# Time-mix preparation of a two-block network on one core: units of k moved among the low-rank products, PSUM banks named by hand, and VectorE's and ScalarE's order rewritten

## The reference, cut to what matters

```python
xs = x[None] + mu[0] * dx_prev + mu[1] * dx_next             # six mixtures of x with its neighbours
r, k, v = einsum('ibld,ide->ible', xs[:3], w_rkv)
lw = tanh(xs[3] @ w1[n]) @ w2[n]                             # n = 0, 1: the two directions, rank 64
decay = exp(-exp(-softplus(-(w0 + lw)) - 0.5))
a = sigmoid(a0 + (xs[4] @ a1[n]) @ a2[n])                    # rank 64
g = sigmoid(xs[5] @ g1) @ g2                                 # rank 160
kk = k * k_k ; kk = kk / max(sqrt(sum over a head of kk*kk), 1e-12)
kd = k * (1 + (a - 1) * k_a)
```

## Time and profile before

| | before |
|---|---|
| median of 3 runs | 2629.68 us |
| profiled execution | 2632.66 us |
| its span | 2630.8 us |
| TensorE busy | 2520.9 us, 96% |
| VectorE busy | 1975.1 us, 75% |
| ScalarE busy | 1532.5 us, 58% |
| mean granted clock of TensorE | 0.981 |

### The profile page before, as it was taken

One profiled execution on the slowest core, in us unless ns is written; L12 is line 12 of the kernel. 1 busy time (PEld: TensorE's weight loads), 2 busy tenths in 40 slices (PEclk: granted clock), 3 DMA queues, 4 the chain that ended last, 5 costly groups with the idle time before them and its releaser, 6 DMA issues. The chain is left out here.

```text
span 2630.8 us, 47726 instructions
## 1 busy us (share of the span) xinstructions
PE 2520.9 (96%) x20277; PEld 2086.0 (79%) x20277; DVE 1975.1 (75%) x2831; ACT 1532.5 (58%) x2229; POOL 175.8 (7%) x192
## 2 busy tenths in 40 slices
PE   8999999999997999999999999999999999999998
PEld 7779997688976667676676767666797999998998
DVE  7855539654445999898999999888586885677874
ACT  5634423422223778787877878786536654437653
POOL 0000000020001260000000000010010201010201
PEclk9989999999999999999999999999999999999999
DMA  7325543330032899999999999997454645444742
GB/s 201 105 65 161 176 161 87 97 96 4 4 112 82 308 388 371 374 376 378 372 367 379 370 374 374 374 367 284 122 164 129 195 148 177 137 143 144 207 137 97
DMA packets 264613, 565.86 MB, mean 215 GB/s; under 512 B 25996, under 2 KB 204356, under 8 KB 221260
## 3 DMA queue, kind: packets, MB, share of 16 engines
q1 hardware_dynamic: 257580, 547.02, 59.2%
q0 software_dynamic: 5248, 10.23, 1.3%
q10 hardware_dynamic: 1568, 5.51, 0.6%
HBM read 545.41 MB, written 11.53 MB: 212 GB/s over the span
## 5 line engine op out<-in xcount | busy, mean ns | idle before, releaser
L319 DVE TENSOR_TENSOR wl<-raw,wh 128x1024 fp32r<-128x1024 f32 (+1 forms) x610 | 741.8, 1223 | 270.6 <-ACT wh L310 254.7
L310 ACT ACTIVATE wh<-raw 128x1024 fp32r<-128x1024 f32 (+1 forms) x610 | 640.7, 1054 | 420.8 <-PE PS L163 405.3
L319 DVE TENSOR_TENSOR wl<-early,wh 128x1024 fp32r<-128x1024 f32 x384 | 467.2, 1232 | 49.7 <-ACT wh L310 31.8
L310 ACT ACTIVATE wh<-early 128x1024 fp32r<-128x1024 f32 x384 | 405.5, 1061 | 121.6 <-PE PS L163 103.7
L161 PE MATMUL PS<-wh,xe_h 128*96 128x512 f32 x896 | 356.2, 398 | 5.2 <-DVE wl L319 3.0
L162 PE MATMUL PS<-wl,xe_h 128*96 128x512 f32 x896 | 352.8, 394 | 0.0
L163 PE MATMUL PS<-wh,xe_l 128*96 128x512 f32 x896 | 352.7, 394 | 0.0
L161 PE MATMUL PS<-b_hn_h,wh 128*128 128x256 f32 (+1 forms) x1152 | 333.0, 289 | 1.4 <-DVE b_t L2887 0.8
L163 PE MATMUL PS<-b_hn_h,wl 128*128 128x256 f32 (+1 forms) x1152 | 327.1, 284 | 0.0
L162 PE MATMUL PS<-b_hn_l,wh 128*128 128x256 f32 (+1 forms) x1152 | 327.1, 284 | 0.0
L161 PEld LDWEIGHTS PS<-b_hn_h,wh 128*128 128x128 f32 (+1 forms) x1152 | 220.6, 192 | 5.7 <-issue 2.7
(11 more groups left out here) (495 smaller groups left out, 4912.4 us busy)
## 6 DMA issues: line engine op xcount, KB each, us to landing
early<-in_moe_in SPq DMA_DIRECT2D x128, 1024.0 KB, 6.8
raw<-in_moe_in SPq DMA_DIRECT2D x96, 1024.0 KB, 7.2
raw<-in_w_in SPq DMA_DIRECT2D x76, 1024.0 KB, 5.5
early<-in_moe_out SPq DMA_DIRECT2D x64, 1024.0 KB, 7.0
raw<-in_moe_out SPq DMA_DIRECT2D x48, 1024.0 KB, 6.1
raw<-in_attn_w_in SPq DMA_DIRECT2D x24, 512.0 KB, 5.5
raw<-in_rw_w_rkv SPq DMA_DIRECT2D x12, 1024.0 KB, 5.2
raw<-in_ffn_w_gate SPq DMA_DIRECT2D x11, 1024.0 KB, 5.2
```

What stands on the lines that cost most here:

```text
L310: act.e.activation(st.two(n)[0], st.raw(n), ACT.Copy).then_inc(*act.sig("hi", st.name, n, sem=f"hi_{st.name}"))
L319: dve.e.tensor_tensor(lo, st.raw(n), hi.bitcast(F32), SUB).then_inc(*dve.sig("lo", st.name, n, sem=f"lo_{st.name}"))
```

## The change

The program is changed in this stage alone. (1) TensorE: `lora_out` makes one column block f at a time, in banks 4 to 7 in turn; units 0 to 3 of k are made behind blocks 1 and 5 of `w_lora` and of `a_lora`, in banks 0 to 3; units 4 to 7 follow, with the head sums 0 to 3 behind them, then the gate's first product, the head sums 4 to 7, and the gate's second product; `k_norm`, `gate_h` 0 and `gate_h` 1 take banks 4, 5 and 6 by name. (2) ScalarE: the exponentials are split in `rate_exps` (KA, fac) and `exps` (KE, RE); the order is squares 0 and 1, both kinds for direction 0, squares 2 and 3, `rate_exps(1)`, `k_part(0)`, squares 4 to 7, `k_part(1)`, Sqrt, `exps(1)`, and then the gate's Sigmoid. (3) VectorE: the scans of `decays` wait for their own column block; two `kk` stand inside each `decays`; `rate(0)`, `kk` 4 and 5, `rate(1)`, `half_k(0, 0)`, `kk` 6 and 7, `half_k(0, 4)` come ahead of the norm, and both halves of direction 1 between the reciprocal and the products of `k_spread`.

43 bank requests (32 low-rank outputs, 8 units of k, `k_norm`, 2 of `gate_h`) no longer move the ring, so everything behind them that takes a bank from the ring gets another one than before.

```diff
-    def unsplit_units(pe, st, event, units, X, Tn, x_event=None):
+    def unsplit_units(pe, st, event, units, X, Tn, x_event=None, at=None):
...
-            b, before = bank(event, i)
+            b, before = bank(event, i, b=at)
...
-        def lora_out(key, x):
+        def lora_out(key, x, f):
...
-            for f in range(KC):
-                for n in range(2):
-                    b, before = bank("lora", key, f, n)
...
+            for n in range(2):
+                b, before = bank("lora", key, f, n, b=4 + (2 * f + n) % 4)
+                pe.wait_ge(pe.at(*before))
...
+            if f == KC - 1:
+                pe.also("direct", "A", m)
+
+        def k_unit(u):
+            unsplit_units(pe, SA, "k", [u], MIXED[1], T, ("mixed", 1), at=u % 4)
...
-        lora_out("w_lora", rw_l)
-        lora_out("a_lora", rw_l2)
-        for u in range(KC + 2):
-            if u == 2:
-                b, before = bank("k_norm")
...
+        for x, (key, y) in enumerate((("w_lora", rw_l), ("a_lora", rw_l2))):
+            for f in range(KC):
+                lora_out(key, y, f)
+                if f in (1, 5):
+                    k_unit(2 * x + f // 4)
+        k_bank, before = bank("k_norm", b=4)
+        pe.wait_ge(pe.at(*before))
+
+        def head_sum(f):
+            pe.wait_ge(pe.at("k_sq", f))
+            e.matmul(PS[0:16, k_bank, 0:T], by_head[:, f, :], rw_q[:, f % 4, :], start=f == 0, stop=f == KC - 1).then_inc(
+                *pe.sig("k_norm_mm", f))
+
+        for u in range(4, KC):
+            k_unit(u)
+            head_sum(u - 4)
...
-            b, before = bank("gate_h", j)
+            b, before = bank("gate_h", j, b=5 + j)
...
+            if j == 0:
+                for f in range(4, KC):
+                    head_sum(f)
...
+        def rate_exps(d):
             act.wait_ge(act.at("decays", d))
             sign = -KAPPA if d == 0 else KAPPA
             e.activation(KA[d], (rw_s if d == 0 else rw_c)[d], ACT.Exp, scale=-sign).then_inc(*act.sig("exp", d, "ka"))
+            e.activation(fac[d], by_chunk(rw_s[d])[:, :, :, CH - 1], ACT.Exp, scale=-KAPPA).then_inc(*act.sig("fac", d))
...
-        for d in range(2):
-            exps(d)
-            for f in range(4 * d, 4 * d + 4):
-                k_square(f)
-            act.wait_ge(act.at("rate_taken", d))
-            for f in range(KC):
...
+        k_square(0)
+        k_square(1)
+        rate_exps(0)
+        exps(0)
+        k_square(2)
+        k_square(3)
+        rate_exps(1)
+        k_part(0)
+        for f in range(4, KC):
+            k_square(f)
+        k_part(1)
         act.wait_ge(act.at("k_norm"))
         e.activation(n16, n16, ACT.Sqrt).then_inc(*act.sig("k_norm_root"))
+        exps(1)
...
-            dve.wait_ge(dve.at("lora", "w_lora", 7, 1))
...
             for f in range(KC):
+                dve.wait_ge(dve.at("lora", "w_lora", f, d))
...
+            for f in (2 * d, 2 * d + 1):
+                kk(f)
+            dve.wait_ge(done)
...
-        for d in range(2):
-            for f in range(4 * d, 4 * d + 4):
-                kk(f)
-            dve.wait_ge(dve.at("lora", "a_lora", 7, 1))
...
-        for d in range(2):
-            half_k(d, 0)
+        rate(0)
+        kk(4)
+        kk(5)
+        rate(1)
+        half_k(0, 0)
+        kk(6)
+        kk(7)
+        half_k(0, 4)
         dve.wait_ge(dve.at("k_norm_mm", KC - 1))
         e.tensor_scalar(n16, ps("k_norm", p=16), 1e-24, None, MAX).then_inc(*dve.sig("k_norm"))
+        e.memset(PAD, 0.0).then_inc(*dve.own())
         dve.wait_ge(dve.at("k_norm_root"))
         e.reciprocal(r16, n16).then_inc(*dve.sig("k_norm_r"))
-        for x in (PAD, XC):
-            e.memset(x, 0.0).then_inc(*dve.own())
+        half_k(1, 0)
+        half_k(1, 4)
+        e.memset(XC, 0.0).then_inc(*dve.own())
...
-        for d in range(2):
-            half_k(d, 4)
```

More of the change, by code:

```diff
@@ L64 @@
             "state scan_zero",
-    "rw_out": "rv k r decays exp prep rate_taken k_part less_ka bonus bonus.kd",
+    "rw_out": "rv k r decays exp fac prep rate_taken k_part less_ka bonus bonus.kd",
     "y_out": "y_mean y_sq y_var y_var_root y_var_r bonus_v y_norm y_gate",
@@ L1021, in lora_out @@
             pe.wait_ge(pe.at("lora_h", key))
-            for f in range(KC):
-                for n in range(2):
-                    b, before = bank("lora", key, f, n)
[L1025 to L1029, removed]
+            for n in range(2):
+                b, before = bank("lora", key, f, n, b=4 + (2 * f + n) % 4)
+                pe.wait_ge(pe.at(*before))
+                t = e.matmul(PS[:, b, 0:T], w2v[64 * n:64 * n + 64, f * 128:(f + 1) * 128], x[64 * n:64 * n + 64, :],
+                             start=True, stop=True)
+                t.then_inc(*pe.sig("lora_mm", key, f, n))
+            if f == KC - 1:
+                pe.also("direct", "A", m)
+        def k_unit(u):
+            unsplit_units(pe, SA, "k", [u], MIXED[1], T, ("mixed", 1), at=u % 4)
         lora_in("w_lora", 3)
         lora_in("a_lora", 4)
-        lora_out("w_lora", rw_l)
-        lora_out("a_lora", rw_l2)
-        for u in range(KC + 2):
-            if u == 2:
-                b, before = bank("k_norm")
[L1038 to L1045, removed]
+        for x, (key, y) in enumerate((("w_lora", rw_l), ("a_lora", rw_l2))):
[12 more added lines that the diff above has]
+            head_sum(u - 4)
         m = SA.of["g1"]
@@ L1283, in lora @@
                         *act.sig("lora", key, f, n))
-        def exps(d):
+        def rate_exps(d):
             act.wait_ge(act.at("decays", d))
@@ L1288, in exps, with k_part @@
             e.activation(KA[d], (rw_s if d == 0 else rw_c)[d], ACT.Exp, scale=-sign).then_inc(*act.sig("exp", d, "ka"))
-            e.activation(fac[d], by_chunk(rw_s[d])[:, :, :, CH - 1], ACT.Exp, scale=-KAPPA).then_inc(*act.own())
-            act.wait_ge(act.last)
+            e.activation(fac[d], by_chunk(rw_s[d])[:, :, :, CH - 1], ACT.Exp, scale=-KAPPA).then_inc(*act.sig("fac", d))
+        def exps(d):
+            sign = -KAPPA if d == 0 else KAPPA
+            act.wait_ge(act.at("fac", d))
             e.activation(KE[d], KE[d], ACT.Exp, scale=sign).then_inc(*act.sig("exp", d, "ke"))
             e.activation(RE[d], RE[d], ACT.Exp, scale=sign).then_inc(*act.sig("exp", d, "re"))
+        def k_part(d):
+            act.wait_ge(act.at("rate_taken", d))
+            for f in range(KC):
+                e.activation(rw_a[d][:, f, 0:T], rw_a[d][:, f, 0:T], ACT.Identity, bias=less_ka[:, f:f + 1],
+                             scale=par("k_a", f)).then_inc(*act.sig("k_part", d, f))
         def k_square(f):
@@ L1303, in rwkv_act @@
         act.wait_ge(act.at("less_ka"))
-        for d in range(2):
-            exps(d)
-            for f in range(4 * d, 4 * d + 4):
-                k_square(f)
-            act.wait_ge(act.at("rate_taken", d))
-            for f in range(KC):
-                e.activation(rw_a[d][:, f, 0:T], rw_a[d][:, f, 0:T], ACT.Identity, bias=less_ka[:, f:f + 1],
-                             scale=par("k_a", f)).then_inc(*act.sig("k_part", d, f))
+        k_square(0)
[9 more added lines that the diff above has]
+        k_part(1)
         act.wait_ge(act.at("k_norm"))
         e.activation(n16, n16, ACT.Sqrt).then_inc(*act.sig("k_norm_root"))
+        exps(1)
         for j, w in enumerate([128, 32]):
@@ L1433, in decays, with rate @@
         def decays(d):
-            dve.wait_ge(dve.at("lora", "w_lora", 7, 1))
             dve.wait_ge(dve.at("c_rw"))
-            dve.wait_ge(dve.last)
             for f in range(KC):
+                dve.wait_ge(dve.at("lora", "w_lora", f, d))
                 e.tensor_tensor_scan(rw_s[d][:, f, :], cst[:, 0:TS], rw_c[d][:, f, :], 0.0, MUL, ADD).then_inc(*dve.own())
-            dve.wait_ge(dve.last)
+            done = dve.last
+            for f in (2 * d, 2 * d + 1):
+                kk(f)
+            dve.wait_ge(done)
             e.tensor_tensor(rw_c[d], rw_s[d], rw_c[d], SUB).then_inc(*dve.sig("decays", d))
+        def rate(d):
+            dve.wait_ge(dve.at("lora", "a_lora", 7, 1))
+            dve.wait_ge(dve.at("exp", d, "ka"))
+            e.tensor_tensor(BE[d], KA[d], rw_a[d], MUL).then_inc(*dve.sig("rate_taken", d))
         def kk(f):
@@ L1456, in rwkv_dve @@
         decays(1)
-        for d in range(2):
-            for f in range(4 * d, 4 * d + 4):
-                kk(f)
-            dve.wait_ge(dve.at("lora", "a_lora", 7, 1))
-            dve.wait_ge(dve.at("exp", d, "ka"))
-            e.tensor_tensor(BE[d], KA[d], rw_a[d], MUL).then_inc(*dve.sig("rate_taken", d))
-        for d in range(2):
-            half_k(d, 0)
+        rate(0)
[6 more added lines that the diff above has]
+        half_k(0, 4)
         dve.wait_ge(dve.at("k_norm_mm", KC - 1))
         e.tensor_scalar(n16, ps("k_norm", p=16), 1e-24, None, MAX).then_inc(*dve.sig("k_norm"))
+        e.memset(PAD, 0.0).then_inc(*dve.own())
         dve.wait_ge(dve.at("k_norm_root"))
```

(5 more changed lines are left out.)

## The result

The changed kernel takes 2652.45 us (median; 2650.56 to 2654.96), the kernel before took 2629.51 beside it (2624.07 to 2630.70): a ratio of 1.0087, 95% interval [1.0071, 1.0103], or some 23 us. The forecast was +8.3 us with a range to 2646. The sign was right, the size was not, and the time lies outside the range. The profiled execution of the changed kernel took 2654.96 with a span of 2652.9 (mean granted clock 0.976, before 0.981).

What follows compares the result with a forecast made beforehand. TensorE, 96% busy, was taken as the bound, with 11 us to win. Preparation +4.5, wave 0 +4.0, s = 0 -5.5, s = 1 +5.3, experts and second block 0 gave +8.3: 2638.0 us, 8-in-10 range 2624 to 2646.

Steps and rivals of the forecast that it cites:

- the three waits: Preparation, TensorE: waits of 4.0 us for k's second load, 5.5 for its third, about 4.5 for the gate's bank.
- the 7.4 us of ScalarE from Sqrt: Preparation: Sqrt, table loads, two exponentials and the gate's copy take 7.4 us while gate_h holds banks k_spread needs.
- the ring in the scan: Scan behind the preparation: later banks turned by three change which holders are waited for, +3.8 us in all.
- wave 0: Scan's start: forward(0), units 6 and 7 of r and back(0) wait for banks, +4.0 us, bounds +2 and +5.
- s = 0: Scan step 0: upd no longer waits 2.70 us and y starts earlier, -5.5 us, bounds -4 and -6.3.
- s = 1: Scan step 1: back(1), forward(2) and y 2 wait for banks, +5.3 us, bounds +3 and +6.
- s = 2: Scan step 2: wins about 0.8 us, as back(2) waits for no res; the later norm loses about as much.
- Preparation, +4.5: Low-rank outputs to r's start: late loads, gate's bank and two clock costs of 1.5 us, +4.5; r at 518.7.
- The upper bound (+6.5): Preparation: a third clock cost after the last wait would make it +6.5 us.
- Experts and second block, 0 (±1): Behind the scan: bank holders differ at a few seams, all long read, so 0 us, bounds -1 and +1.
- loses nothing: Preparation, VectorE: half_k(1) and memsets, 6.5 us of work, fit while k_spread waits for the gate's bank, costing nothing.
- The rival with the loads in time: Preparation: k's second and third loads come in time, r at 506.7, -7.2 us; 2626.3 in all; chance 0.12.

Runs made afterwards that it cites:

- 14 profiles: Profiles of the kernel before and the changed kernel, two each, and of the follow-up kernels: eight with the ring turned, six with it as before.
- the turned profiles: The eight profiles of kernels whose ring of banks stayed turned; r to the scan's end took mean 245.3 us, from there to the end 1876.7.
- the second pair: Changed kernel and kernel before, each run unchanged once more for a second profile: 2648.78 us (1.0083) and 2627.20 us (1.0001).
- run 9: Changed kernel with 3, 5 and 3 idle TensorE products put into its three waits: 2644.27 us, 1.0061.
- runs 1: Changed kernel with the ring moved by three ahead of k_spread, restoring the banks of the kernel before from there on: 2638.62 us, 1.0038.
- run 2: Changed kernel with exps(1) put behind the gate's two Sigmoids on ScalarE, ring still turned: 2645.98 us, 1.0063.
- run 8: Changed kernel with the ring moved by three only behind k_spread, so the gate's hold on its banks stays: 2645.86 us, 1.0056.
- run 5: Changed kernel with ring restored ahead of k_spread, gate's Sigmoids before exps(1), and k's units 2 and 3 behind a_lora's last block: 2626.49 us, 0.9987.
- 6: The kernel of run 5 with VectorE's two half_k(1) products moved behind its be and ke products: 2620.51 us, 0.9962.
- Run 4: Changed kernel with k's units 2 and 3 moved behind a_lora's last block, none among a_lora's blocks: 2634.94 us, 1.0025.

## Why the prediction was wrong

Right, by its own steps: the sign; the three waits and their causes; the 7.4 us of ScalarE from Sqrt; the table loads at 1.28 us; the ring in the scan, +3.8 forecast against 3.4 over 14 profiles. There each part moved the way that was said. From r to the first product of `res`, and then from each step's first `res` to the next, the means of the turned profiles differ by +4.6 (wave 0), -4.5 (s = 0), +5.4 (s = 1) and -1.8 (s = 2), against +4.0, -5.5, +5.3 and -0.8.

Wrong, two terms:

*Preparation, +4.5.* The step that failed is the price of the half clock. The part measured +11.8 (12.4 in the second pair, 12.0 in both from the first low-rank output on), and r came 7.0 us beyond the 518.7 of the working. Along TensorE's row: `w_lora`'s tail ends 1.2 us later than my pace for four banks gave, and blocks 2 to 7 of `a_lora` with unit 3 take 0.8 more, 2.0 in all. The clock makes the rest. I added 1.5 to unit 2 and it was 1.9 (5.62 less 3.7), added 1.5 to unit 4 and it was 2.9, and left the spreads at full clock, where 28 of their matmuls take 6.61 instead of 3.42 (run 9), 3.2 more: 5.0 us beyond what I allowed. I took the clock's price from the one wait of the earlier trace rows, 2.80 us, and used it for forecast waits of 4.0 and 5.5. The upper bound (+6.5) added one more such price, where the third stretch alone costs 3.2 ahead of r and 2.9 in r's first four units (17.80 against 14.93 in run 9). Nor is the price one number: behind a wait of 3.2 to 3.3 us unit 2 took 5.62 in both profiles of the changed kernel, but 6.22, 6.92 and 6.85 in runs 1, 2 and 8, against 3.93 at full clock. Run 9 shows the term as a cause of its own. The Trainium skill describes this pattern, a wait for a DMA that lowers the clock of the products behind it (TensorE: Matmul & The Clock Gate, "HAM oscillation — how this bites in real kernels"); the two stretches behind the loads agree, at 0.54 and 0.51. The third stretch followed no DMA but a wait for ScalarE.

*Experts and second block, 0 (±1).* The step that failed is that the holders there are all long read. Over 14 profiles it is +5.4 behind the scan. 1.5 us of it are shown: `out` 3 of the second block waits for VectorE's read of the bank of `out` 0, in each of the eight turned profiles and in none of the six others. Another wait, of 0.5 us, lies ahead of the norm behind the time mix in the same eight and in no other; I had set it, at 0.8, against s = 2. No other wait there is found in all of the turned profiles and in none of the others. Of the remaining 3.4 us some 3.1 are half clock: summed over the clock that each trace grants behind the scan, the turned profiles lose 30.1 us (23.6 to 35.0) and the others 27.0 (23.8 to 30.6). These ranges overlap widely, so whether the ring brings that clock or chance does stays open.

One statement was wrong and cost nothing here: that VectorE "loses nothing" by `half_k(1)` ahead of the spreads. It held only under the gate's wait; run 2 has it bare, with 2.24 us of waiting, and in run 5 it is 1.83. Runs 5 and 6 differ by 3.5 us in r's start and by 6.0 in time (2626.49 against 2620.51), of which the move itself explains those 1.8.

The rival with the loads in time failed by the very rows that were put against it. Run 4, in another order of the units, comes nearest to it: r at 512.57, not 506.7. Sqrt starts at 498.55 and not 495.8, and the rival's sum had the gate's wait but not the clock of the spreads, 3.2 us.

Accounting: 12.0 of the preparation, 1.2 of r's first units at half clock, 3.4 and 5.4 of the ring: 22.0 of 22.9 us. That it comes so near is partly luck, as single profiles scatter by some us behind r.

## What to carry to other kernels

Before products are interleaved, follow the weights' slots: a product that is moved past others delays the load that takes its slot, and a 1 MB load (5.2 us here) then stands open. Price a wait of TensorE at its length and at the half clock behind it, and give that price a range: here full units behind a wait of 3.2 to 3.3 us lost 1.7 to 3.0, the one behind 5.3 us lost 2.9, and the 16-row spreads with r's units behind 3.2 us lost 6.1. Where banks are taken from a ring, naming a bank turns the ring for everything that comes later: give the turns back, or follow the holders to the last block.

## What the runs showed of the hardware

- The low clock outlasted the work it first hit. At the gate's 3.20 us (and the spreads after it, 16 rows each) the granted clock was 0.51 over 14 us, 6 us into r's full products; at 3.29 us ahead of full products it was 0.54 over 3.75, at 5.32 us 0.51 over 7.
- A wait of nearly the same length did not cost the same in every execution: unit 2 took 5.62 us behind 3.29 and 3.25 us, 6.85 behind 3.24 us (run 8), 6.92 behind 3.16 us (run 2), and 3.93 at full clock.
- Eleven products whose results nobody reads (3, 5 and 3) kept the clock at 1.00 through all three waits and brought r forward by 6.5 to 7.5 us in a kernel that is otherwise the same.
- A product of 128 x 512 in float32 took 0.90 us, in two records of 0.45.
- Two profiles of one kernel agree within 0.1 us from the first low-rank output to r (78.32 and 78.31; 66.28 and 66.28), and differ by up to 8 us over the 240 us behind it (245.7 and 237.9). Half clock explains at most 5.1 of these (8.5 us lost against 3.4); the rest is open.
